# Making modulation blocks on VectorE instead of TensorE in a two-layer trunk, with MLP loops written out and norms applied by a diagonal matrix

## The chip, the cores and the metric

The kernel runs on one core of one Trainium2 chip. The metric is the device time of one execution in microseconds (us); lower is better.

## What is computed

Two layers over 256 latent tokens of width 2048 (D), with 256 context tokens that feed layer 0 alone:

```python
for i in range(2):
    m_lat = split(silu(c)     @ ada_w[i] + ada_b[i], 6)   # shift, scale, gate; shift, scale, gate
    m_ctx = split(silu(c_ctx) @ ada_w[i] + ada_b[i], 6)   # layer 0 only
    hn = rms_norm(h, norm1_g[i]) * (1 + m_lat[1]) + m_lat[0]
    if i == 0:   # one projection (6560 columns) for both head groups, then one output projection
        y = concat(diff_attention(hn @ w_in), rwkv7(hn @ w_in)) @ w_out
    else:        # pointwise 2048->4096, gate, 31-tap depthwise convolution, norm, silu, pointwise
        y = conformer_conv(hn)
    h = h + m_lat[2] * y
    hn = rms_norm(h, norm2_g[i]) * (1 + m_lat[4]) + m_lat[3]
    h = h + m_lat[5] * (square(relu(hn @ mlp_w1[i])) @ mlp_w2[i])
```

The modulation `silu(c) @ ada_w` has 6 chunks of 2048 columns per layer, worked on in blocks of 512 columns: 48 blocks in all, each with 2048 x 512 weights (4 MB). The context's row is needed for layer 0's first two chunks alone.

## The kernel before, in words

All work is written out per engine; each engine runs its queue in order and waits on semaphores. The stages, with their place in the profiled execution: 8 modulation blocks and the first norm (0 to 143 us); the input projection, 13 products of up to 512 columns (143 to 616); 8 attention heads, one modulation block each (650 to 820); the RWKV recurrence, 8 passes of two heads (837 to 1590), called heads here; the output projection, 4 products (1607 to 1697); layer 0's MLP (1718 to 2440); layer 1's convolution module (2468 to 2857), MLP (from 2881) and store.

**Products.** A product's weights come in 4 chunks of 1 MB into `raw`, from SP's queue. ScalarE rounds a chunk into `split_hi` (`act_split`), VectorE subtracts for `split_lo` (`dve_split`), TensorE multiplies. All three buffers are single: a chunk's load waits for both splits of the same chunk of the product before, ScalarE's split for TensorE's end with that chunk of the product before. So ScalarE's split of the last chunk starts when TensorE ends a product. In the input projection ScalarE then evicts banks 0 and 1, VectorE 2 and 3, and ScalarE stores all of them. A chunk takes TensorE 10.9 us, or 5.4 in products 0, 1, 6 and 7.

**Modulation blocks.** The weights are moving operand, the vector `s32` of 32 columns stationary; `pe_ada_chunk` (L361) does four matmuls of a chunk side by side into four partition groups, whose sum is made later by the loads that read it. `act_ada` (L377) copies the bank and stores 4 rows in `mod_scratch`. Blocks 16 to 47 are done in the recurrence, 4 per head: `ada_chunk` at steps 8, 12, 18 and 22 of the inverse (28 steps of transposes L1272, updates L1229, mask L962 on VectorE, copies L728 and L732 on ScalarE) and 12 in the scan (four parts; L1285, L1313, L1330, L1349, L1350, L1298; VectorE L1065). Between the scan's parts work of the next head is done (`rates`, `decays`, `key_norm`, `decay_sums`, `turn`); `scaled_queries` (L921, L924) is VectorE's last work for the next head's first scores (L1212). L1236, the mean of the head before, stands just ahead of these.

**Gates.** Pool makes `gate` (128 x 2048) from the bias and four partition groups, each a load of 1 MB that accumulates and waits for the one before: five loads for each gate, issued when the products that used the gate before have been added (`res_add`). VectorE waits for it (`gate_in`) before the MLP's first split of a next product.

**MLP.** Four quarters, each 4 up products (`pe_joined`, L438 and L440) and 4 down products (`pe_product`, L420), in a hardware loop (`Fori`) on PE, ACT, DVE and SP; layer 1's last quarter is written out on ACT and DVE alone. An up product is evicted by ScalarE (a half copy), VectorE (sum, squared relu, low part), a down product by VectorE (times gate, add to `hbuf`).

**Norms.** `act_stats` squares both token tiles (128 x 2048) with a sum, takes the root; `dve_scale` scales the tiles into `xn2`; TensorE transposes 8 groups of four (L455); `dve_modulate` applies gain and shift; ScalarE and VectorE split.

Of the kernel before, what the change touches and what calls it, by code (L numbers as in the profile page):

```python
# [14 lines left out]
P = 128  # L15
# [113 lines left out]
ADA_A, ADA_T, ADA_R = 8, 1, 4  # L129
Q_AT = ADA_A  # L130
Q_RW = Q_AT + ADA_T * HEADS
Q_ALL = Q_RW + ADA_R * HEADS
# [102 lines left out]
def build_trunk(nc, a, out):  # L235
    with ExitStack() as top:
# [20 lines left out]
        part = line[:, 2:4, :]  # L257
        s32 = sb(top, "s32", [P, KT, 32])
# [11 lines left out]
        epsc = sb(top, "epsc", [P, 2])  # L270
        prow = [hbuf[:, 0, 0:P], hbuf[:, 0, P:2 * P]]
# [6 lines left out]
        with ExitStack() as s:  # L278
# [8 lines left out]
            xa_hi, xa_lo = xa[:, :, 0, :], xa[:, :, 1, :]  # L287
            with ExitStack() as t:
                hT_hi = sb(t, "hT_hi", [P, KT, SEQ], F32R)
                hT_lo = sb(t, "hT_lo", [P, KT, SEQ], F32R)  # L290
            with ExitStack() as t:
                xn2 = sb(t, "xn2", [P, 2, D])
# [15 lines left out]
        ST_T = 16 * HEADS  # L308
        ST_END = [ST_T + 16 * HEADS * (ADA_R // 2), 16 * HEADS * (ADA_R // 2)]
# [6 lines left out]
        norm_sq = sem("norm_sq")  # L316
# [18 lines left out]
        def send(sp, src, n, before):  # L335
# [10 lines left out]

        def rwkv_ada(i, j):

            return (0, i.n(NB, Q_RW * NB)) if j == 0 else (1, i.n((ADA_R - 1) * NB, (j - 1) * NB))

# [30 lines left out]
        def act_split(act, m, b, n=NB):  # L381

            for c in range(NCH):
                act.wait_ge(raw_in[c], b * 16 + 16)
                if not (isinstance(m, int) and m == 0):
                    act.wait_ge(pe_chunk, m * 4 + (c - 3))
                nc.scalar.activation(split_hi[:, c, :, 0:n], raw[:, c, :, 0:n], ACT.Copy).then_inc(hi_done, 1)  # L387

# [68 lines left out]

        def dve_modulate(dve, n0, tiles, cols, hi, lo):
# [54 lines left out]
        def load_mod_rows(pool, m, layer, col):  # L513

            for g in range(4):
                pool.dma_start(mrow[32 * g:32 * g + 32, m, :], rows_of(mod_d[layer, g, col:col + 2 * D])).then_inc(mrow_in, 16)
# [5 lines left out]
        def gate_part(pool, n, l, c, g):  # L522

            pool.wait_ge(gate_in, n * 80 + (g + 1) * 16)
# [39 lines left out]
        def evacuated(m, bank):  # L564

            mine = 0 if bank < 2 else 2
            return sum(1 for n in range(m + 1) for b, *_ in mix_out(n) if mine <= b < mine + 2 and (n < m or b <= bank))

# [80 lines left out]
        def rwkv_act(act, steps):  # L649
# [68 lines left out]
            def ada_rows(x, j):  # L718

                layer, col = rwkv_ada(x, j)  # L720
                slot = 1 - j % 2
                act_ada(act, layer, col, x.n(ADA_R, Q_RW + j), slot, x.n(32, (ST_T, 0)[slot] + 16 * (j // 2)), 0)

# [10 lines left out]
            def scan(x, last):  # L734

                for c in range(4):
# [4 lines left out]
                    if c == 0:  # L741
                        ada_rows(x, 0)
                        if not last:
                            rates(x.next())
                    elif c == 1:
                        if not last:
                            decays(x.next())
                        ada_rows(x, 1)
                        if not last:
                            key_norm(x.next())  # L750
# [3 lines left out]
                    else:  # L754
                        ada_rows(x, 2)
# [4 lines left out]
                ada_rows(x, 3)  # L760
# [373 lines left out]
        def rwkv_pe(pe):  # L1134
# [9 lines left out]
            def ada_chunk(x, n):  # L1144

                j, c = divmod(n, NCH)
                q = x.n(ADA_R, Q_RW + j)
                pe_ada_chunk(pe, q, x.n(ADA_R, Q_RW + MIX_M + j), c, 0, q)

# [106 lines left out]
            def inverse(x, first):  # L1256
# [7 lines left out]
                for k in range(NS + 2):  # L1264
# [13 lines left out]
                    elif k in (8, 12, 18, 22):  # L1278
                        ada_chunk(x, (8, 12, 18, 22).index(k))
# [21 lines left out]
            def scan(x, last):  # L1301
# [6 lines left out]
                for c in range(4):  # L1308
# [9 lines left out]
                    elif c == 1:  # L1318
                        ada_chunk(x, 6)
                        if not last:  # L1320
                            decays(x.next(), 1)
                    elif c == 2:
                        if not last:
                            decay_sums(x.next(), 0)
                        ada_chunk(x, 9)
# [8 lines left out]
                    if c == 0:  # L1334
                        ada_chunk(x, 4)
                    elif c == 1:
                        ada_chunk(x, 7)
                    elif c == 2:
                        if not last:
                            decay_sums(x.next(), 1)  # L1340
                        ada_chunk(x, 10)
                    else:
                        ada_chunk(x, 12)
# [12 lines left out]
                    if c == 0:  # L1356
                        if not last:
                            decays(x.next(), 0)
                        ada_chunk(x, 5)
                    elif c == 1:  # L1360
                        if not last:
                            key_norm(x.next())
                        ada_chunk(x, 8)
                    elif c == 2:
                        if not last:
                            decay_sums(x.next(), 2)
                        ada_chunk(x, 11)
                    else:
# [5 lines left out]
                if not last:  # L1374
                    for n in range(1, 5):
# [41 lines left out]
        diag_a, diag_used = sem("diag_a"), sem("diag_used")  # L1417
        TR0, TR1, TR2 = 16, 24, 32
# [12 lines left out]

        def sync_rest(sp):
# [3 lines left out]

            def mlp(l, m0):
                with sp.Fori(0, Q4) as i:
                    for k in range(4):
                        send(sp, weight_src(a["mlp_w1"][l], i * D + k * NB), NB, src(i * 8 + (m0 + k)))  # L1440
                    for k in range(4):
                        send(sp, weight_src(a["mlp_w2"][l], k * NB, NB, i * D), NB, src(i * 8 + (m0 + 4 + k)))
# [13 lines left out]
        def pool_rest(pool):  # L1456
            stage_end(pool, 3)

            for b in range(2):
                pool.wait_ge(ada_st[b], ST_END[b])  # L1460
            pool.dma_start(line[0:1, 1, :], a["conv_pw2_b"][:, NB:2 * NB]).then_inc(line_in, 16)
# [737 lines left out]
```

## Time and profile before

| | us |
|---|---|
| median of 3 runs | 3624.95 (3624.19 to 3635.03) |
| the profiled execution, its own time | 3620.88 |
| its span, first to last instruction | 3619.2 |
| TensorE busy (PE) | 3290.5 (91%) |
| VectorE busy (DVE) | 1890.1 (52%) |
| ScalarE busy (ACT) | 1364.8 (38%) |
| mean granted TensorE clock | 0.952 of 2.4 GHz |

The profile is one execution recorded by the hardware. PE is TensorE, DVE VectorE, ACT ScalarE, SP and POOL the two engines that issue most of the DMAs; L361 is line 361. In a timeline row stand start, duration, engine, line, operation, what is written and read, count, and in brackets the idle time of the engine before it and what ended that. An fp32 matmul leaves two records, a transpose one. The granted clock is 1.00 at 2.4 GHz and 0.50 at 1.2 GHz.

### The profile page before, as it was taken

What the parts mean: (1) busy time and instruction counts of PE and PEld (TensorE: products, weight loads), DVE (VectorE), ACT (ScalarE), POOL (GpSimd) and SP (SyncE); (2) the same over time, 40 slices, a digit from 0 to 9 for tenths busy, and PEclk for the clock granted to TensorE, in tenths of its full rate; (3) what the DMA queues carried; (4) which work ended last, traced back from release to release, by engine and by line L of the source; (5) the groups of instructions that cost most, each with busy time, mean ns of one, the idle gap of its engine ahead of it and who ended that gap; (6) DMA issues with size and microseconds to landing.
All of it is one profiled execution on the core that took longest, in us unless ns stands there. A gap on an engine that the chain in (4) does not pass through costs nothing.

```text
span 3619.2 us, 48320 instructions
## 1 busy us (share of the span) xinstructions
PE 3290.5 (91%) x19488; PEld 2668.8 (74%) x19488; DVE 1890.1 (52%) x2244; ACT 1364.8 (38%) x1581; POOL 91.3 (3%) x148
## 2 busy tenths in 40 slices
PE   5799998567999999978999999997998899999999
PEld 1588986235777777746888888887986677878787
DVE  0522321666556555535555555555996555555554
ACT  1321220334555555533333343333463333434342
POOL 1000000010000000000000000000000000000000
PEclk8799999678999999989999999998999999999999
DMA  9633531684555555565655655556521565565553
GB/s 357 219 128 127 163 110 51 239 250 136 191 196 195 197 197 193 188 249 189 182 195 184 197 186 189 184 194 180 186 82 58 168 193 194 178 198 175 189 179 132
DMA packets 320206, 651.07 MB, mean 180 GB/s; under 512 B 15499, under 2 KB 20321, under 8 KB 316641
## 3 DMA queue, kind: packets, MB, share of 16 engines
q1 hardware_dynamic: 300000, 597.04, 49.1%
q0 software_dynamic: 8896, 35.95, 4.2%
q10 hardware_dynamic: 11104, 15.01, 1.2%
q8 instruction: 169, 2.77, 0.3%
q14 instruction: 37, 0.30, 0.0%
HBM read 634.22 MB, written 13.60 MB: 179 GB/s over the span
## 4 chain that ended last, share of the span: by engine, by line
PE 83%; DMA 7%; DVE 6%; issue 2%; ACT 1%; ACTq 1%; POOL 0%; SPq 0%; POOLq 0%; DVEq 0%
PE ps L420 42%; PE ps L438 13%; PE ps L440 6%; PE ps L1229 6%; DMA raw<-in_ada_w_dram 4%; PE ps L361 3%; PE ps L1272 3%; PE ps L1785 2%; DMA gate<-mod_scratch 2%; DVE rw_scl L944 1%; PE ps L2167 1%; PE ps L1285 1%; DMA at_qk<-qkv_scratch 1%; PE ps L1330 1%; DVE rw_scc L947 1%
## 5 line engine op out<-in xcount | busy, mean ns | idle before, releaser
L397 DVE TENSOR_TENSOR split_lo<-raw,split_hi 128x2048 fp32r<-128x2048 f32 (+1 forms) x372 | 850.0, 2288 | 1095.3 <-ACT split_hi L387 1049.6
L387 ACT ACTIVATE split_hi<-raw 128x2048 fp32r<-128x2048 f32 (+1 forms) x372 | 710.3, 1911 | 1323.8 <-PE ps L420 974.0
L438 PE MATMUL ps<-xa,split_hi 128*128 128x512 f32 x2048 | 724.7, 398 | 21.2 <-DVE split_lo L397 12.2
L440 PE MATMUL ps<-xa,split_lo 128*128 128x256 f32 x2048 | 576.3, 281 | 9.3 <-issue 9.3
L438 PEld LDWEIGHTS ps<-xa,split_hi 128*128 128x128 f32 x2048 | 388.3, 190 | 125.7 <-issue 35.5
L420 PE MATMUL ps<-split_lo,hT_hi 128*128 128x512 f32 x1024 | 398.4, 389 | 0.0
L420 PE MATMUL ps<-split_hi,hT_lo 128*128 128x512 f32 x1024 | 398.4, 389 | 0.0
L420 PE MATMUL ps<-split_hi,hT_hi 128*128 128x512 f32 x1024 | 398.4, 389 | 0.0
L440 PEld LDWEIGHTS ps<-xa,split_lo 128*128 128x128 f32 x2048 | 390.5, 191 | 0.0
L361 PE MATMUL ps<-raw,s 128*32 128x512 f32 x1536 | 224.3, 675 | 49.4 <-DMA raw<-in_ada_w_dram 49.3
L420 PEld LDWEIGHTS ps<-split_hi,hT_hi 128*128 128x128 f32 x1024 | 192.2, 188 | 40.2
L420 PEld LDWEIGHTS ps<-split_lo,hT_hi 128*128 128x128 f32 x1024 | 192.2, 188 | 39.8
L420 PEld LDWEIGHTS ps<-split_hi,hT_lo 128*128 128x128 f32 x1024 | 192.2, 188 | 39.7
L1229 PEld LDWEIGHTS ps<-rw_tt,rw_mx 128*128 128x128 f32 x1536 | 187.1, 192 | 29.8 <-ACT rw_mx L732 29.2
L1229 PE MATMUL ps<-rw_tt,rw_mx 128*128 128x128 f32 x1536 | 206.4, 278 | 0.0
L728 ACT ACTIVATE rw_tt<-ps 128x512 f32<-128x512 f32 x224 | 133.7, 597 | 164.6 <-PE ps L1229 164.6
L420 PE MATMUL ps<-xa,split_hi 128*128 128x256 f32 x1024 | 186.2, 285 | 6.2 <-DVE tmpa L476 6.2
L420 PE MATMUL ps<-split_hi,xa 128*128 128x512 f32 x512 | 163.0, 398 | 31.0 <-DVE split_lo L397 19.3
L962 DVE TENSOR_TENSOR rw_mb<-rw_tt,rw_lmask 128x512 f32<-128x512 f32 x192 | 132.4, 689 | 96.5 <-ACT rw_tt L728 96.3
L420 PEld LDWEIGHTS ps<-xa,split_hi 128*128 128x128 f32 x1024 | 161.3, 194 | 6.5 <-issue 6.5
L420 PE MATMUL ps<-mx_lo,split_hi 128*128 128x512 f32 (+1 forms) x448 | 157.4, 351 | 0.0
L420 PE MATMUL ps<-mx_hi,split_hi 128*128 128x512 f32 (+1 forms) x448 | 157.3, 351 | 0.0
(328 smaller groups left out, 4408.0 us busy)
## 6 DMA issues: line engine op xcount, KB each, us to landing
raw<-in_mlp_w_dram SPq DMA_DIRECT2D x256, 1024.0 KB, 5.3
raw<-in_ada_w_dram SPq DMA_DIRECT2D x192, 1024.0 KB, 8.1
raw<-in_mix_in_w_dram SPq DMA_DIRECT2D x48, 1024.0 KB, 5.1
raw<-in_conv_pw_w_dram SPq DMA_DIRECT2D x48, 1024.0 KB, 5.2
gate<-mod_scratch POOLq DMA_DIRECT2D x16, 1024.0 KB, 8.3
raw<-in_mix_out_w_dram SPq DMA_DIRECT2D x16, 1024.0 KB, 5.8
qkv_scratch<-hbuf ACTq DMA_DIRECT2D x20, 256.0 KB, 3.8
rwkv_scratch<-hbuf ACTq DMA_DIRECT2D x18, 256.0 KB, 2.2
```

Of the source, the lines that this page charges most:

```text
L361: mm = pe.matmul(ps[32 * kk:32 * kk + 32, ADA_ACC[acc], :], s32[:, c * CHUNK + kk, :], raw[:, c, kk, :], start=(c == 0), stop=(c == NCH - 1))
L387: nc.scalar.activation(split_hi[:, c, :, 0:n], raw[:, c, :, 0:n], ACT.Copy).then_inc(hi_done, 1)
L397: nc.vector.tensor_tensor(split_lo[:, c, :, 0:n], raw[:, c, :, 0:n], split_hi[:, c, :, 0:n], ALU.subtract).then_inc(lo_done, 1)
L420: mm = pe.matmul(dst, l, r, start=(first and i == 0 and opens), stop=(last and i == 2), skip_group_check=True)
L438: pe.matmul(ps[:, base + j, :], split_hi[:, c, kk, j * P:(j + 1) * P], both, start=(k == 0), stop=False, skip_group_check=True)
L440: mm = pe.matmul(ps[:, base + j, 0:SEQ], split_lo[:, c, kk, j * P:(j + 1) * P], xa_hi[:, k, :], start=False, stop=(k == KT - 1), skip_grou ...
L728: nc.scalar.activation(rw["tt"][:, k % 4, :, :], four(ZB[k % 4]), ACT.Copy).then_inc(W["z7"], 1)
L944: ins = V.tensor_tensor(rw["scl"][:, c - 2, inst, :].rearrange("p (q t) -> p q t", q=4), ps[:, SCB[n], :].rearrange("p (q t) -> p q t", q= ...
L962: V.tensor_tensor(dh(rw["mb"][:, k % 2, :, :]), dh(src), bc(rw["lmask"][:, lev, :, :], 2), ALU.mult).then_inc(W["mb"], 1)
L1229: mm = pe.matmul(ps[:, ZB[c], inst * P:(inst + 1) * P], R["mx"][:, k % 2, inst, :], rhs, start=(k < 4 and inst == 0), stop=True, skip_grou ...
L1272: tr = pe.transpose(ps[:, MB[k % 2], inst * P:(inst + 1) * P], R["mb"][:, k % 2, inst, :], ident[:, :])
L1785: mm = pe.matmul(ps[:, j // 2, (j % 2) * SEQ:(j % 2 + 1) * SEQ], diag[:, t % DIAG_SLOTS, j, :], gpad[:, KT - PE_F + j, t:t + SEQ], start=( ...
```

## The change

Four things.

1. The 32 blocks of the recurrence go. Sixteen (layer 0's chunks 4 and 5, layer 1's 0 and 1) are made on VectorE during the input projection, sixteen (layer 1's chunks 2 to 5) during layer 0's MLP. A block is 16 steps on a piece of 128 x 512 (256 KB, one DMA each from SP's queue): `acc = piece * scale + acc` (`piece_step`, `late_step`), each waiting for the one before. Then four small matmuls with ones add up the partitions (`sum_rows`, `late_sum`) at a set chunk of a set product, into the first bank of the next product in the projection; ScalarE copies and stores the row (`keep_rows`, `late_rows`). By the tables `M_STEPS` and `L_STEPS` there are 7 steps a chunk (3 in products 0, 1, 6 and 7) in the projection, 9 a product in the MLP until its 29th. Sums in the projection come before chunks (1,3), (2,3), (3,1), (3,3), (4,1), (5,0), (5,2), (6,0), (7,0), (8,1), (9,0), (9,2), (10,0), (10,3), (11,1), (11,3) (product, chunk); in the MLP before chunk 2 of 16 of the products. Pieces have 7 buffers in the projection and 3 in the MLP.
2. These blocks have one row, not four, so three of the four gates and most modulation rows need one load after the bias, not four.
3. The MLPs are written out on all engines.
4. A norm takes its squares block by block beside the products before it; TensorE multiplies `hbuf` by a diagonal matrix of the reciprocal deviations (`pe_scaled_turns`) in place of scaling and transposing.

```diff
-ADA_A, ADA_T, ADA_R = 8, 1, 4
+ADA_A, ADA_T = 8, 1
+ADA_M, M_BUF = 16, 7
+ADA_L, L_BUF = 16, 3
...
+        def pe_scaled_turns(pe, n0):
+            for i in range(KT // 2):
+                n = n0 + i
+                if n >= 4:
+                    pe.wait_ge(tr_ts, n - 3)
+                for j in range(2):
+                    for t in range(2):
+                        k = 2 * i + j
+                        o = (2 * j + t) * P
+                        mm = pe.matmul(ps[:, n % 4, o:o + P], hbuf[:, t, k * P:(k + 1) * P], rdiag[:, t, :], start=True, stop=True)
+                mm.then_inc(tr_ps, 1)
...
+        def act_squares(act, steps, k, count):
+            act.wait_ge(res_add, count)
+            for t in range(2):
+                steps.link(nc.scalar.activation(sqj[:, :], hbuf[:, t, k * NB:(k + 1) * NB], ACT.Square,
+                                                accum_out=small[:, 18 + 4 * t + k:19 + 4 * t + k]))
...
+        M_STEPS = [0]
+        for m in range(MIX_M):
+            for c in range(NCH):
+                M_STEPS.append(min(M_STEPS[-1] + (3 if m in (0, 1, 6, 7) else 7), ADA_M * KT))
+        M_SUM = {}
+        for b in range(ADA_M):
+            M_SUM[next(j for j in range(len(M_STEPS)) if M_STEPS[j] >= (b + 1) * KT) + 1] = b
...
+        def piece_step(dve, n):
+            b, k = divmod(n, KT)
+            acc, scale = macc[:, b % 2, :], s32[:, k, 0:1]
+            dve.wait_ge(piece_in[n % M_BUF], 16 * (n // M_BUF + 1))
...
+                dve.wait_ge(macc_ok, n)
+                nc.vector.scalar_tensor_tensor(out=acc, in0=piece[n % M_BUF], scalar=scale, in1=acc,
+                                               op0=ALU.mult, op1=ALU.add).then_inc(macc_ok, 1)
...
+        def sum_rows(pe, m, b):
+            pe.wait_ge(macc_ok, (b + 1) * KT)
+            if m >= 1:
+                pe.wait_ge(mix_ev_a, evacuated(m - 1, 0))
+            pe.wait_ge(mrow_ok, b)
+            pe_partition_sums(pe, mix_bank(m + 1, 0), macc[:, b % 2, :]).then_inc(mrow_ps, 1)
...
+        def keep_rows(act, m, b):
+            layer, col = mix_ada(b)
+            act.wait_ge(mrow_ps, b + 1)
+            act.wait_ge(mrow_st, 16 * b)
+            nc.scalar.activation(mline, ps[:, mix_bank(m + 1, 0), 0:P], ACT.Copy).then_inc(mrow_ok, 1)
+            act.wait_ge(mrow_ok, b + 1)
+            store_rows(act, layer, col, mline).then_inc(mrow_st, 16)
...
-                    elif k in (8, 12, 18, 22):
-                        ada_chunk(x, (8, 12, 18, 22).index(k))
...
-                        ada_chunk(x, 13)
                 if not last:
-                    turn(x.next(), 0)
-                ada_chunk(x, 14)
-                ada_chunk(x, 15)
-                if not last:
-                    for n in range(1, 5):
+                    for n in range(5):
                         turn(x.next(), n)
...
+        L_STEPS = [0]
+        for t in range(NCH * 32):
+            L_STEPS.append(min(L_STEPS[-1] + (3 if t % NCH == 0 else 2), ADA_L * KT))
...
+        def load_late(sp, n):
+            b, k = divmod(n, KT)
+            if n >= L_BUF:
+                sp.wait_ge(macc_ok, MIX_STEPS + n - L_BUF + 1)
+            sp.dma_start(lpiece[n % L_BUF], ada_src(1, 2 * D + b * NB)[:, k, :]).then_inc(piece_in[n % L_BUF], 16)
...
+        def late_sum(pe, m, b):
+            i, k = divmod(m, 8)
+            pe.wait_ge(macc_ok, MIX_STEPS + (b + 1) * KT)
+            if k == 0:
+                pe.wait_ge(res_ps, 4 * i + 3)
+                pe.wait_ge(tr_ts, TR0 + 8)
+            elif k < 6:
+                pe.wait_ge(sum_ok, 4 * i + min(k, 4))
+            else:
+                pe.wait_ge(res_ps, 4 * i + 5)
...
                 for c in range(NCH):
                     if m + 1 < MIX_M:
                         dve_split_chunk(dve, m + 1, c, min(NB, IN_COLS - (m + 1) * NB))
+                    for n in range(M_STEPS[4 * m + c], M_STEPS[4 * m + c + 1]):
+                        piece_step(dve, n)
...
                 def bank_free(g, m=m, banks=banks):
+                    if g == 0 and m:
+                        pe.wait_ge(mrow_ok, sum(1 for t in M_INSIDE if t < 4 * m))
...
-            with act.Fori(0, Q4) as i:
-                mlp_quarter(i, M_MLP0, 0, 4, False)
+            for i in range(Q4):
+                mlp_quarter(i, M_MLP0, 0, 4, False, True)
```

## Rows read from the trace of the kernel before

**Rows 1.** The page's part 4: the chain that ended last, by engine.
```profile
PE 83%; DMA 7%; DVE 6%; issue 2%; ACT 1%; ACTq 1%; POOL 0%; SPq 0%; POOLq 0%; DVEq 0%
```

**Rows 2.** Timeline of PE in one head's inverse; then the page's part 5.
```profile
1059.57 0.60 PE L1272 MATMUL ps<-ident_t,rw_mb 128*128 128x128 f32 x4
1060.10 1.06 PE L361 MATMUL ps<-raw,s 128*32 128x512 f32 x8
1062.09 0.60 PE L1272 MATMUL ps<-ident_t,rw_mb 128*128 128x128 f32 x4
1063.42 0.60 PE L1272 MATMUL ps<-ident_t,rw_mb 128*128 128x128 f32 x4
...
L728 ACT ACTIVATE rw_tt<-ps 128x512 f32<-128x512 f32 x224 | 133.7, 597 | 164.6 <-PE ps L1229 164.6
```

**Rows 3.** PE before MLP products: timeline; waits (idle us, count, longest) of 1750:2430, 2930:3619.
```profile
1746.30 0.77 PE L438 MATMUL ps<-xa,split_hi 128*128 128x512 f32 x1 [5.60 <-DVE split_lo L397]
...
PE ps L438 <- issue: 5.9, 6, 1.3
...
PE ps L440 <- issue: 9.3, 3, 3.2
```

**Rows 4.** Timeline of ACT, then of PE, at layer 0's second norm.
```profile
1704.05 1.91 ACT L494 ACTIVATE xn<-hbuf 128x2048 f32<-128x2048 f32 x1 [4.75 <-DVE hbuf L1585]
...
1711.11 4.27 PE L455 MATMUL ps<-ident_t,xn 128*128 128x128 f32 x24 [13.82 <-DVE xn L504]
```

**Rows 5.** One line's instructions: min/median/max ns, first and last start; then PE's timeline.
```profile
L1236 PE MATMUL ps<-rw_o,rw_blk x16: 379/380/483, 947.0 to 1583.8; 128*128 128x256 f32 x16
...
1550.59 1.10 PE L1285 MATMUL ps<-rw_vt,rw_scc 128*128 128x64 f32 x8 [0.69 <-ACT rw_tt L728]
```

**Rows 6.** Timeline of DVE, then of PE, at the end of a scan.
```profile
1121.02 0.42 DVE L1065 TENSOR_TENSOR rw_u<-ps,rw_rh 128x256 f32<-128x256 f32 x1 [2.69 <-PE ps L1330]
...
1128.25 0.42 DVE L924 TENSOR_TENSOR rw_kx<-rw_r,rw_ep 128x256 f32<-128x256 f32 x1
...
1130.71 0.50 PE L1212 MATMUL ps<-rw_kx,rw_bh 64*128 64x128 f32 x4
```

**Rows 7.** Windows: length, busy us (count) PE PEld DVE ACT POOL, PEclk, DMA, GB/s.
```profile
1554.00:1557.00 3.00, 3.00 (x24) 1.22 (x25) 0.00 (x0) 0.00 (x0) 0.00 (x0) 0.50 0.00 0
3254.00:3260.00 6.00, 5.55 (x18) 4.77 (x18) 1.07 (x1) 0.00 (x0) 0.00 (x0) 0.50 0.55 175
1746.30:1751.30 5.00, 5.00 (x15) 4.29 (x16) 5.00 (x3) 0.00 (x0) 0.00 (x0) 0.50 0.80 262
1711.00:1714.00 3.00, 2.89 (x14) 2.89 (x15) 1.79 (x5) 0.63 (x1) 0.17 (x1) 0.50 0.78 117
1714.00:1718.00 4.00, 2.42 (x19) 1.94 (x18) 3.78 (x8) 1.66 (x3) 0.00 (x0) 0.99 0.85 174
```

**Rows 8.** Timeline of DVE: one multiply-add, and a split.
```profile
1121.37 0.74 DVE L904 SCALAR_TENSOR_TENSOR rw_kk<-rw_k,rw_cur,rw_t 128x512 f32<-128x512 f32 x1
...
1743.63 8.90 DVE L397 TENSOR_TENSOR split_lo<-raw,split_hi 128x2048 fp32r<-128x2048 f32 x4 [17.86 <-DMA gate<-mod_scratch]
```

**Rows 9.** Timeline of ACT at the end of a projection product.
```profile
363.32 1.91 ACT L387 ACTIVATE split_hi<-raw 128x2048 fp32r<-128x2048 f32 x1 [8.96 <-PE ps L420]
365.13 1.06 ACT L1911 ACTIVATE hbuf<-ps 128x512 f32<-128x512 f32 x2
```

**Rows 10.** Windows of the opening and of layer 0's MLP, columns as in 7.
```profile
20.00:100.00 80.00, 59.13 (x284) 16.50 (x284) 6.51 (x10) 9.33 (x14) 0.00 (x0) 0.78 1.03 374
1760.00:2430.00 670.00, 664.11 (x3349) 562.90 (x3348) 364.40 (x196) 258.31 (x151) 0.00 (x0) 1.00 0.58 189
```

**Rows 11.** DMA issues: transfer, queue, count, KB each, median us to landing.
```profile
raw<-in_mlp_w_dram SPq DMA_DIRECT2D x256, 1024.0 KB, 5.3
raw<-in_ada_w_dram SPq DMA_DIRECT2D x192, 1024.0 KB, 8.1
at_cos<-in_cos_dram ACTq DMA_DIRECT2D x1, 256.0 KB, 2.6
```

More of the change, by code:

```diff
@@ L257, in build_trunk @@
         part = line[:, 2:4, :]
+        piece = [gate[:, b * NB:(b + 1) * NB] for b in range(4)] + [tmpa[:, b, :] for b in range(2)] + [line[:, 3, :]]
+        macc, mline = line[:, 0:2, :], line[:, 2, 0:P]
         s32 = sb(top, "s32", [P, KT, 32])
@@ L511, in mod_columns, with parts_of, load_mod_rows @@
             mm.then_inc(mt_ps, 1)
[L513 to L516 removed]
+        def parts_of(layer, chunk):
+            return 4 if (layer, chunk) in PARTED else 1
+        def load_mod_rows(pool, m, layer, chunk):
+            for o in range(2):
+                for g in range(parts_of(layer, chunk + o)):
+                    r0, col = 32 * g + 16 * o, (chunk + o) * D
+                    pool.dma_start(mrow[r0:r0 + 16, m, :], rows_of(mod_d[layer, g, col:col + D])).then_inc(mrow_in, 16)
+        GATES = [(0, 2), (0, 5), (1, 2), (1, 5)]
+        GATE_END = [sum(16 + 16 * parts_of(*x) for x in GATES[:n + 1]) for n in range(4)] + [0]
         def gate_bias(pool, l, c):
@@ L567, in evacuated, with mix_ada, pe_partition_sums, store_rows @@
             return sum(1 for n in range(m + 1) for b, *_ in mix_out(n) if mine <= b < mine + 2 and (n < m or b <= bank))
+        def mix_ada(b):
+            return (0, (16 + b) * NB) if b < 8 else (1, (b - 8) * NB)
+        def pe_partition_sums(pe, bank, acc):
+            for g in range(4):
+                mm = pe.matmul(ps[32 * g:32 * g + 32, bank, 0:P], ones[:, 0:32], acc[:, g * P:(g + 1) * P], start=True, stop=True)
+            return mm
+        def store_rows(act, layer, col, rows):
+            return act.dma_start(mod_d[layer, 0, col:col + NB].rearrange("(g n) -> g n", g=4), rows[0:P:32, :])
@@ L754, in scan @@
                     else:
-                        ada_rows(x, 2)
                         if not last:
@@ L1333, in scan @@
                         mm = inputs_of(x, c + 1)
[L1334 to L1343, printed above, removed]
+                    if c == 2 and not last:
+                        decay_sums(x.next(), 1)
                     pe.wait_ge(W["u"], x.n(4, c + 1))
@@ L1417, in build_trunk @@
         diag_a, diag_used = sem("diag_a"), sem("diag_used")
+        MROW_LOADS = sum(parts_of(l, c + o) for l, c in ((0, 3), (1, 0)) for o in range(2))
         TR0, TR1, TR2 = 16, 24, 32
@@ L1547, in act_rest @@
                 act_split(act, M_PW2 + n + 1, M_PW2 + n + 1 + B_OFF)
+                if n:
+                    act_squares(act, steps, n - 1, 20 + n)
             norm(3, TR2)
-            with act.Fori(0, Q4 - 1) as i:
-                mlp_quarter(i, M_MLP1, 16, 24, False)
-            mlp_quarter(Q4 - 1, M_MLP1, 16, 24, True)
+            for i in range(Q4):
+                mlp_quarter(i, M_MLP1, 16, 24, i == Q4 - 1)
         def dve_rest(dve, steps):
@@ L1622, in dve_rest @@
             norm(1, TR0, 0)
-            dve.wait_ge(gate_in, 160)
-            with dve.Fori(0, Q4) as i:
+            dve.wait_ge(gate_in, GATE_END[1])
+            for i in range(Q4):
                 mlp_quarter(i, M_MLP0, 0, 4, False)
@@ L1741, in mlp, with rows_kept, free @@
             def mlp(m0, abase, rbase, tr0):
-                with pe.Fori(0, Q4) as i:
-                    for k in range(4):
-                        def free(k=k):
+                for i in range(Q4):
+                    for k in range(8):
+                        r = 8 * i + k
+                        def rows_kept(r=r):
+                            if m0 == M_MLP0 and sum(1 for x in L_SUM if x < r):
+                                pe.wait_ge(mrow_ok, ADA_M + sum(1 for x in L_SUM if x < r))
+                        def free(i=i, k=k):
+                            rows_kept()
                             if k == 0:
@@ L1833, in _, with pieces @@
                 n = min(NB, IN_COLS - m * NB)
-                send(sp, weight_src(w["in"], m * NB, n), n, ("product", m - 1) if m else ("ada", ADA_A - 1))
+                def pieces(c, m=m):
+                    if m == 1 and c == 0:
+                        sp.wait_ge(tr_lo, 16)
+                        sp.wait_ge(col_ps, ADA_A)
+                        sp.wait_ge(pt_ok, 1)
+                        for k in range(M_BUF):
+                            load_piece(sp, k)
+                    elif m > 1:
+                        t = 4 * (m - 2) + c
+                        for k in range(M_STEPS[t] + M_BUF, min(M_STEPS[t + 1] + M_BUF, ADA_M * KT)):
+                            load_piece(sp, k)
+                send(sp, weight_src(w["in"], m * NB, n), n, ("product", m - 1) if m else ("ada", ADA_A - 1), pieces)
+            for k in range(M_STEPS[4 * (MIX_M - 2)] + M_BUF, ADA_M * KT):
+                load_piece(sp, k)
             sp.wait_ge(hi_done, 4 * MIX_M)
```

250 lines of the change are left out of this document (170 added, 80 removed).

## The prediction

> **What bounds the kernel now.** I read the page first. TensorE holds 83% of the chain that ended last [rows 1]. So a change pays where it takes work from TensorE or closes one of its pauses, and costs where it makes TensorE wait. Next, the timeline of one head of the recurrence: TensorE goes from one instruction to the next without a pause, a step of the inverse takes 1.33 us (1062.09 to 1063.42), and the step with a modulation chunk 2.52 us (1059.57 to 1062.09) [rows 2]. Then the pauses of TensorE outside: 5.60 us at the second product of layer 0's MLP (and 6.64 at the same place of layer 1's, the second of two such rows), about 1 to 3 us at each loop turn of the MLPs [rows 3], 13.8 us before the transposes of a norm, of which there are three [rows 4]. VectorE has time to spare, but the moved work must fit into its gaps in the projection and in layer 0's MLP.
>
> **A. 32 blocks leave the recurrence.** A head takes (1583.8 - 947.0) / 7 = 91.0 us [rows 5] and holds 16 chunks. Four in the inverse cost 2.52 - 1.33 = 1.19 each, 4.8 us: without them ScalarE's two copies (0.60 each [rows 2]) still fit into 1.33. Eight in the scan's first three parts cost 1.0 each (the chunk's 1.06 less its overlap with the next [rows 2]); what follows was always ready earlier, except once behind ScalarE's square root: 7.7 us. At the scan's end VectorE takes over: from its sum at 1121.02 to its last product, over at 1128.67, run 7.65 us, and the next scores can't start earlier; today they come 9.7 us after that sum [rows 6]. That part gives 2.0 us, not 4. Together 14.5 us a head, times 7. The last head has nothing of a next head to fill its scan. It runs 32.9 us from 1550.59 to 1583.4 [rows 5], the last chunks waiting for their DMA. I count its instructions with 0.7 us for each hop over ScalarE or VectorE: 20.4 us, so 12.5 less, plus 4.8 in the inverse, minus 4 for the clock: it fell to half right there, at 1554 to 1557, after two short waits [rows 7]. **A = -(101.5 + 13.3) = -115.** Bounds: every chunk free and every DMA wait gone, -135; only half of each scan chunk and nothing at the end, -70.
>
> **B. 16 blocks in the projection.** The multiply-add has its shape in the trace: 0.74 us, and 0.03 until one that needs it can start, 0.775 a step [rows 8]. A full chunk gets 7: 5.4 + 2.2 for the split = 7.6 us of VectorE against 10.9 of TensorE; a 256-column chunk or one of the first two products gets 3: 4.5 against 5.4. That fits. The waits don't. A sum is a matmul set in TensorE's queue, and the bank it writes is freed by an eviction that ScalarE does only after the split of the last chunk, which TensorE's own end of product releases: start 363.32, evicted at about 365.7, TensorE's chunk before ended at about 363.1, so 2.5 us [rows 9]. By the code's tables five sums stand at chunk 0 (products 5, 6, 7, 9, 10) and wait for that; five at chunk 3 (1, 2, 3, 10, 11), and the next product then waits for ScalarE's copy of them, behind the same split: 2.35 us, one more after the others. With the first sum late by up to 7 us, since its pieces start late, and 16 sums at 0.3 us (between nothing, beside other work, and 1.0, an old chunk), that is 11 x 2.4 + 3 + 4.8 = 34 us. Pauses of this size lower the clock sometimes: after one of 3.2 us it was at half from 3254 to 3260 [rows 7]; I add 8. VectorE's piece steps also stand ahead of its evictions, for whose end ScalarE's stores wait; with three chunks in hand the splits stand that. **B = +42**, from +20 (pauses half as long, no clock) to +60.
>
> **C. 16 blocks in layer 0's MLP.** A product lasts about 22 us. VectorE has 4 splits (8.9 [rows 8]), two or three operations over half a split's columns (1.2 each), and now 9 steps (7.0): 18.3 to 19.5 us, 86%, from 54% [rows 10]. DMA goes from 189 GB/s to 189 + 2.36 MB / 22 us = 296, against 374 in the opening, where it is full [rows 10]. Only three buffers hold pieces: a load is issued when the step three before is done, and lies in one queue behind 1 MB of weights. A 1 MB load lands in 5.3 us, a 256 KB one alone in 2.6 [rows 11]; behind the other I reckon 5.3 + 0.7 and then 0.7 more for the second, 6.0 and 6.7 us. VectorE wants the first of them about 6.2 us after the split while on time, but 3.8 to 4.6 once it is late, so it can't catch up after each eviction. Followed through chunk by chunk this gives 1 to 3 us of waiting a product; VectorE then needs 21 to 23 us against 22, and TensorE waits at its sums, which ask for VectorE's eviction of the product before. **C = +27** (4.8 for the sums, 22 for waits), from +5, all hidden, to +65, at 0.7 us longer landings and less speed.
>
> What a piece costs in flight is also in the Trainium skill ("DMA: Bandwidth & Descriptors", Anatomy of one DMA): some 2.0 us fixed, plus the bytes. As an estimate from that page a 256 KB piece is 2.7 us, and my sum would be the same; the 2.6 us row agrees.
>
> **D. The gates.** In both MLPs VectorE stood before the gate's parts (17.86 us in layer 0), and TensorE then idled 5.60 and 6.64 [rows 3, 8]. With one part instead of four the gate is there some 25 us earlier. Behind it nothing is late: the norm ends before. The clock was at half for some 5 us after each [rows 7], which costs 2.6. **D = -17.4**; bounds -12 and -18.
>
> **E. Loops written out.** TensorE's pauses at turns are all put down to issue: 5.9 us in six pauses in layer 0; in layer 1 three long ones of 9.3 us together and three short ones like layer 0's, 3. The clock fell after two of the long ones, 5 us [rows 3, 7]. The projection is written out and shows no such pause. **E = -23**, at worst -8 if fetching instructions beside more DMA costs again.
>
> **F. Norms.** From the first square (1704.05) to the transposes (1711.11) 7.1 us: two squares of 1.9, root, reciprocal, two scalings of all of x [rows 4]. Now one block's squares, a quarter of that and their fixed part (2 x 0.9), root, and two small scalings: 3.6 us. The matmul costs two passes where the transpose has one, so the first group comes 0.9 us later, more at the low clock. **F = -6** for three, between -10 and +1.
>
> The Trainium skill ("TensorE: Matmul & The Clock Gate", Part 4) says that transposes don't count as activity for the clock; by it matmuls instead would bring the clock up sooner and F would be nearer -10. The trace speaks against it: with nothing but transposes run, the clock went from 0.50 to 0.99 within the norm [rows 7]. F stands as it is.
>
> **Nothing** for the small loads of modulation rows, the squares on ScalarE (idle 60% of the MLP) and the start of the output projection: there the load of x, issued after the yT copies, is last to arrive in both versions.
>
> **Sum**: -115 + 42 + 27 - 17 - 23 - 6 = -92. The profiled execution took 3620.9 us (span 3619.2), 4 below the median of 3625.0; against the mean of both I predict **3531 us**.
>
> **Rivals.** (1) *The clock falls in every scan.* The old chunks were TensorE's densest work there; the last head shows a fall. Against it: seven heads keep the next head's work as filling. Price: some 8 us a head, 56: 3587. Chance 0.08. (2) *The scan's chain of hops sets the pace*: the chunks hid it, each is worth half. A is -75: 3571. 0.10. (3) *Slower than before*: with three buffers a round of three steps lasts a landing plus a step. If, in the fuller queue, pieces land like the 1 MB modulation loads did, 8.1 us [rows 11], a product with its three rounds takes 3 x 8.9 = 26.7 us, 4.7 more over 28.4 products: C = +134, 3638. It decides from about 6.5 us of landing on (22 / 3 less a step), and reaches the old time near 7.9. 0.07. (4) *Little of B and C shows*: 20 and 5 us: 3487. 0.13. The forecast, 3500 to 3565, has the rest, 0.62.
>
> The skill's same page warns ("Why this matters for your kernels") that pauses between bursts of matmuls take the clock down; that is rival 1, which removing filling invites. If it held for every scan the time would be the 3587 above.
>
> **How the numbers follow.** The range leaves out rival 3 and the edge of rival 4: 3483 to 3592. A measurement can tell about 0.3%, 11 us, from no change. Slower: 0.07. Within: 0.03, between rivals 2 and 3. Faster: 0.90.
>
> **What would show it.** A: heads of 77 us, TensorE waiting for VectorE's last scaled query at their end. B: eleven pauses of 2.4 us at product edges. C: VectorE's steps waiting for DMA, TensorE's for sums, a stage longer by 20 us. D and E: no pauses at the second products and at quarter edges. F: 3.6 us in place of 7.1. It is wrong if the granted clock falls in the heads, if heads stay above 80 us, or if layer 0's MLP grows past 60 us.

## The result, and the profile after

The changed kernel takes 3597.23 us (median of four runs, 3593.53 to 3598.71) against 3628.34 for the kernel before beside it. The ratio is 0.9915, 95% interval 0.9898 to 0.9932: about 0.85% faster, some 31 us, where 92 were forecast. The two profiled executions differ by 22.6 us of span (3619.2 and 3596.6), and the table takes that apart. A stage lasts from TensorE's first instruction of its kind to the first of the next.

| stage | before | after | difference | the prediction had |
|---|---|---|---|---|
| projection, up to attention | 507.6 | 552.9 | +45.3 | +42 (B) |
| attention | 185.5 | 191.2 | +5.6 | 0 |
| recurrence, up to the output projection | 770.4 | 662.5 | -108.0 | -115 (A) |
| output projection, up to norm 1's transposes | 103.9 | 99.2 | -4.8 | part of F |
| norm 1, layer 0's MLP, up to norm 2 | 743.1 | 802.0 | +58.9 | +13 (C 27, part of D and E -14), part of F |
| norm 2, convolution module, up to norm 3 | 420.3 | 420.0 | -0.3 | part of F |
| norm 3, layer 1's MLP, end | 744.7 | 725.1 | -19.6 | -26 (rest of D and E), part of F |

Of the 69 us between -92 and -22.6, some 46 lie in one stage: layer 0's MLP. First the page of the changed kernel: the chain that ended last by engine (before: rows 1), the group of the late multiply-adds with its idle time, and the loads of pieces with their median time to landing.

```profile
PE 66%; DMA 13%; DVE 13%; issue 5%; ACT 2%; ACTq 1%; SPq 0%; POOL 0%; POOLq 0%; DVEq 0%
...
L1541 DVE SCALAR_TENSOR_TENSOR line<-line,cvec 128x512 f32<-128x512 f32 x160 | 119.9, 750 | 96.8 <-DMA line<-in_ada_w_dram 91.1
...
line<-in_ada_w_dram SPq DMA_DIRECT2D x207, 256.0 KB, 5.5
```

TensorE's share of the chain fell from 83 to 66%, and DMA and VectorE rose to 13% each. Now the changed kernel's windows, columns as in rows 7: the projection, one head, the last head's scan, layer 0's MLP, layer 1's MLP.

```profile
143.75:662.45 518.70, 492.79 (x2432) 409.69 (x2432) 309.74 (x329) 106.56 (x88) 0.00 (x0) 0.98 0.70 246
982.50:1059.64 77.14, 72.45 (x654) 64.43 (x653) 54.64 (x106) 44.76 (x82) 4.77 (x8) 1.00 0.05 13
1496.66:1525.52 28.86, 24.22 (x185) 20.81 (x185) 4.60 (x15) 1.53 (x4) 0.00 (x0) 0.60 0.01 1
1658.54:2441.66 783.12, 735.95 (x3715) 616.94 (x3713) 563.44 (x474) 290.74 (x223) 0.00 (x0) 0.96 0.75 254
2880.50:3596.60 716.10, 710.28 (x3587) 601.99 (x3585) 386.27 (x217) 269.88 (x160) 0.00 (x0) 1.00 0.56 179
```

Three stages hold idle time and low clock that the kernel before has not to this degree: layer 0's MLP, where TensorE is busy for 736 of 783 us at a mean clock of 0.96; the projection, 493 of 519 us at 0.98; and the last scan, at 0.60 (0.95 before, 1550.59 to 1583.40). TensorE's timeline shows what idles: two of eleven pauses in the projection, the transposes of norm 1, two of eight long pauses in the MLP. Behind them VectorE's and SyncE's timelines of one down product, in which late pieces show.

```profile
193.77 0.47 PE L430 MATMUL ps<-split_hi,mx_hi 128*128 128x512 f32 x1 [2.43 <-ACT line L684]
336.31 0.43 PE L633 MATMUL ps<-line,ones_t 128*32 128x128 f32 x8 [2.59 <-issue]
1649.49 9.29 PE L478 MATMUL ps<-rdiag,hbuf 128*128 128x128 f32 x64 [9.72 <-DVE rdiag L503]
1768.61 0.66 PE L633 MATMUL ps<-line,ones_t 128*32 128x128 f32 x8 [7.16 <-DVE tmpa L1772]
1889.60 0.66 PE L633 MATMUL ps<-line,ones_t 128*32 128x128 f32 x8 [7.89 <-issue]
```

```profile
1999.15 2.29 DVE L407 TENSOR_TENSOR split_lo<-raw,split_hi 128x2048 fp32r<-128x2048 f32 x1
2002.70 1.61 DVE L1541 SCALAR_TENSOR_TENSOR line<-line,cvec 128x512 f32<-128x512 f32 x2 [1.27 <-DMA line<-in_ada_w_dram]
2004.23 2.28 DVE L407 TENSOR_TENSOR split_lo<-raw,split_hi 128x2048 fp32r<-128x2048 f32 x1
2006.43 0.75 DVE L1541 SCALAR_TENSOR_TENSOR line<-late,cvec,line 128x512 f32<-128x512 f32 x1
2008.45 0.75 DVE L1541 SCALAR_TENSOR_TENSOR line<-line,cvec 128x512 f32<-128x512 f32 x1 [1.27 <-DMA line<-in_ada_w_dram]
2009.12 2.29 DVE L407 TENSOR_TENSOR split_lo<-raw,split_hi 128x2048 fp32r<-128x2048 f32 x1
2011.32 0.75 DVE L1541 SCALAR_TENSOR_TENSOR line<-line,cvec 128x512 f32<-128x512 f32 x1
2014.68 0.75 DVE L1541 SCALAR_TENSOR_TENSOR line<-late,cvec,line 128x512 f32<-128x512 f32 x1 [2.62 <-DMA late<-in_ada_w_dram]
2015.35 1.22 DVE L1744 TENSOR_TENSOR tmpa<-ps,gate 128x1024 f32<-128x1024 f32 x1
```

```profile
2006.59 0.38 SPq L355 DMA_DIRECT2D raw<-in_mlp_w_dram  x1
2007.20 0.33 SPq L1528 DMA_DIRECT2D late<-in_ada_w_dram  x1
```

VectorE waits three times in this product, 5.2 us together, each time for a piece. The load of the last `late` piece is issued at 2007.20, when the step three before is over, and its multiply-add starts at 2014.68, 7.5 us on; this landing is a long one, the median is 5.5. The evictions (L1744) come behind that wait, and the sums on TensorE (L633) behind the evictions: the row at 1768.61 names VectorE's L1772, and the "issue" of 7.89 us at 1889.60 ends when the same L1772, begun at 1888.28 and 1.22 us long, is over.

The heads came out as forecast. One line of the source view answers rows 5, one line of TensorE's waits (total, count, longest) names what is last at a head's end:

```profile
L1338 PE MATMUL ps<-rw_o,rw_blk x16: 379/382/794, 982.5 to 1526.1; 128*128 128x256 f32 x16
...
PE ps L1314 <- DVE rw_kx L1032: 7.0, 7, 1.0
```

Six of the seven distances between means are 77.1 to 77.2 us, at full clock; the last is 80.1.

### The profile page after: what moved, and what is told of

Same layout as the page of the kernel before. It is cut to its first block, busy times and chain, and to the rows that moved or that the text cites. A ratio compares the mean times of both kernels' runs of the same rounds, so it can differ in the third digit from the quotient of the medians.

```text
span 3596.6 us, 46596 instructions
## 1 busy us (share of the span) xinstructions
PE 3223.9 (90%) x18816; PEld 2689.8 (75%) x18816; DVE 2240.7 (62%) x2761; ACT 1367.6 (38%) x1653; POOL 81.3 (2%) x136
## 4 chain that ended last, share of the span: by engine, by line
PE 66%; DMA 13%; DVE 13%; issue 5%; ACT 2%; ACTq 1%; SPq 0%; POOL 0%; POOLq 0%; DVEq 0%
PE ps L430 35%; PE ps L448 7%; PE ps L1331 6%; DMA late<-in_ada_w_dram 5%; DMA line<-in_ada_w_dram 4%; PE ps L450 4%; DVE line L1541 3%; PE ps L1374 3%; DMA raw<-in_ada_w_dram 2%; PE ps L1972 2%; ACT split_hi L395 1%; PE ps L1385 1%; PE ps L1428 1%; DVE rw_scl L1052 1%; PE ps L2383 1%
## 5 line engine op out<-in xcount | busy, mean ns | idle before, releaser
L448 PE MATMUL ps<-xa,split_hi 128*128 128x512 f32 x2048 | 735.8, 403 | 0.0
L430 PE MATMUL ps<-xa,split_hi 128*128 128x256 f32 x1024 | 186.7, 285 | 5.7 <-DVE tmpa L524 5.7
L1541 DVE SCALAR_TENSOR_TENSOR line<-line,cvec 128x512 f32<-128x512 f32 x160 | 119.9, 750 | 96.8 <-DMA line<-in_ada_w_dram 91.1
```

The costliest lines, as they stand in the source:

```text
L430: mm = pe.matmul(dst, l, r, start=(first and i == 0 and opens), stop=(last and i == 2), skip_group_check=True)
L448: pe.matmul(ps[:, base + j, :], split_hi[:, c, kk, j * P:(j + 1) * P], both, start=(k == 0), stop=False, skip_group_check=True)
L1541: nc.vector.scalar_tensor_tensor(out=acc, in0=lpiece[n % L_BUF], scalar=scale, in1=acc, op0=ALU.mult, op1=ALU.add).then_inc(macc_ok, 1)
```

## The experiments

The question was what holds up layer 0's MLP, then what the projection, the loops and the last scan each cost. All but one were run once, beside the kernel before; stages are read from their traces. How much a stage scatters shows where the code is the same: norm to norm, layer 0's MLP took 802.0 us in the changed kernel and 805.8 and 797.0 in experiments 7 and 10, which don't touch it.

**1. No loads.** In layer 0's MLP each buffer is loaded once; the steps read it again and again.

```diff
-            sp.dma_start(lpiece[n % L_BUF], ...).then_inc(piece_in[n % L_BUF], 16)
+            if n < L_BUF:
+                sp.dma_start(lpiece[n % L_BUF], ...).then_inc(piece_in[n % L_BUF], 16)
```

> The changed kernel with the pieces of layer 0's MLP loaded only three times, once into each buffer; every multiply-add and every sum stays, so the kernel leaves out the true weights of layer 1's last four modulation chunks. From the first transposes of the norm before this MLP to those of the norm behind it the stage takes 802 us in the changed kernel, 743 before. Theory (pieces land too late): VectorE's 152 us of waiting for pieces make it late at the sums; without them the eight pauses of 3.4 to 8.5 us (46.5 together) and the falls of the clock behind them go, and the stage takes 740 to 752. Rival 1 (VectorE's work is too much as it is, 19 us of 22): the stage stays above 780. Rival 2 (the sums stand too early, whatever VectorE waits for): about half of the pauses stay, 770.

Measured: 3531.9 us; norm to norm 735.3. In the window of the MLP (columns as in rows 7) TensorE is never idle and the clock is full:

```profile
1661.23:2377.42 716.19, 716.19 (x3715) 602.30 (x3713) 565.15 (x474) 292.55 (x223) 0.00 (x0) 1.00 0.57 185
```

All 256 multiply-adds and 16 sums are still there. So neither VectorE's work nor the sums' place costs anything to speak of alone; the waits for pieces, with what follows from them, cost 67 us. Both rivals fall.

**2. Sums one chunk later.**

```diff
-                            if m0 == M_MLP0 and c == 2 and r in L_SUM:
+                            if m0 == M_MLP0 and c == 3 and r in L_SUM:
```

> The changed kernel with each sum of layer 0's MLP before chunk 3 of its product, not chunk 2; pieces load as before. TensorE then gives VectorE 5.4 us more. Theory (VectorE with its waits is slower than TensorE, so it falls back until something stops TensorE): the pauses move or shrink little, the stage takes 785 to 802. Rival (only the sums' place is wrong): pauses of 3.4 to 8.5 us lose 5.4 each, the stage takes 755 to 765.

Measured: 3585.1 us; the stage 795.0, with 16 pauses of together 40.5 us in place of 9 of 47.2. Five of them, 7.8 us together, are new waits of the next product for ScalarE's copy of the row, which now stands behind a later split; some of the others now stand before the splits. The 7 us gained are little more than the scatter. TensorE is stopped by VectorE's pace, and a later sum mostly moves where: the rival falls.

**3. A fourth buffer.** A piece may be loaded into `s32`, not used any more by then; the squares' scratch moves to `rdiag`, the summed row's to a small buffer of its own.

```diff
-ADA_L, L_BUF = 16, 3
+ADA_L, L_BUF = 16, 4
...
-            lpiece = [line[:, 2, :], line[:, 3, :], late[:, :]]
+            lpiece = [line[:, 2, :], line[:, 3, :], late[:, :], s32[:, :, :].rearrange("p k n -> p (k n)")]
```

> The changed kernel with four buffers for pieces in layer 0's MLP, not three. Theory (pieces land too late): a load is issued one step earlier, some 2.4 us, VectorE's 152 us of waiting fall under 40, and the stage falls from 802 to 740 to 760. Rival (DMA's throughput, not its latency, is the limit): the waits stay over 100 and the stage over 785.

Measured: 3526.2 us; the stage 735.1 and no pause. VectorE's waits in that stretch, of the changed kernel and then of this one (total, count, longest; the buffer `s` is the fourth), and this one's window of the MLP:

```profile
DVE line L1541 <- DMA line<-in_ada_w_dram: 91.1, 56, 3.8
DVE line L1541 <- DMA late<-in_ada_w_dram: 53.4, 25, 4.7
```

```profile
DVE line L1543 <- DMA line<-in_ada_w_dram: 18.4, 15, 3.4
DVE line L1543 <- DMA late<-in_ada_w_dram: 10.1, 8, 3.8
DVE line L1543 <- DMA s<-in_ada_w_dram: 9.7, 9, 1.7
...
1655.14:2371.30 716.16, 716.16 (x3715) 602.63 (x3713) 564.11 (x474) 292.62 (x223) 0.00 (x0) 1.00 0.82 278
```

The same bytes come in less time, 278 GB/s in place of 254, though a single piece now lands later (median 6.4 to 6.7 us in that stretch, not 5.5). So it was the time of one landing against too few buffers, not throughput.

**4. Two buffers.**

```diff
-ADA_L, L_BUF = 16, 3
+ADA_L, L_BUF = 16, 2
```

> The changed kernel with two buffers for pieces in layer 0's MLP, not three. Theory (latency of one round): two steps need at least a landing and a step, 5.5 + 0.75 = 6.25 us, so 9 steps of a product need 28 us and more against 22, and the stage between the norms grows from 802 to 900 to 980. If the waits were one of throughput, two buffers would load no more bytes and the stage would stay under 830.

Measured: 3689.6 us; the stage 892.7, a little under the forecast. Pieces landed sooner with fewer in flight, in a median of 5.0 us, where the forecast had put 5.5. The stage by buffers: 892.7 with two, 802.0 with three, 735.1 with four, 735.3 without loads.

**5. The same steps at a lower rate**, three buffers.

```diff
-            L_STEPS.append(min(L_STEPS[-1] + (3 if t % NCH == 0 else 2), ADA_L * KT))
+            L_STEPS.append(min(L_STEPS[-1] + (3 if t % 16 == 0 else 2), ADA_L * KT))
```

> The changed kernel, three buffers, with the same 256 steps of layer 0's MLP spread over 31 products, 8.25 each, not 9 over 28.4. Theory (the round sets VectorE's pace): in the changed kernel's trace one buffer's steps follow each other every 7.7 us (five rounds from 1998.5 to 2037.1), so 9 steps need 3 x 7.7 = 23.1 us and TensorE's product takes some 22.3; 8.25 need 21.2, VectorE catches up, and the stage between the norms falls from 802 to 740 to 765. Rival (each step carries its own wait of 0.6 us, whatever the rate): the same sum of waits, 790 to 802.

Measured: 3558.2 us; the stage 765.9, pauses 23.6 us. But the waits stayed:

```profile
DVE line L1541 <- DMA line<-in_ada_w_dram: 90.0, 59, 3.3
DVE line L1541 <- DMA late<-in_ada_w_dram: 47.2, 29, 3.5
```

My theory, by which three rounds of 7.7 us set VectorE's pace, falls: VectorE did not catch up and the waits did not vanish, as the rival said, while the time was nearer to mine. What does add up in both kernels is VectorE's time for one product. Four splits (9.2), the eviction (3.6, the mean of up and down products, with the wait for ScalarE's half), 9 steps (6.8) and 152 us of waits over 28.4 products (5.4) make 24.9 us; measured, (802.0 - 735.1) / 28.4 = 2.4 over TensorE's 22.3, which is 24.7. With 8.25 steps and 145 us over 31 products it is 9.2 + 3.6 + 6.2 + 4.7 = 23.7; measured 22.3 + (765.9 - 735.1) / 31 = 23.3. The waits in these sums are read from the traces, so they account for the pace and don't forecast it. A reading that fits, and is argued only: as long as the sum is over 22.3, VectorE stays late, and a late VectorE asks for every piece too soon.

**6. Pieces from a queue of their own**, GpSimd's, so that none stands behind a 1 MB chunk in SyncE's.

```diff
+                if n == 4:
+                    pool.wait_ge(mt_ps, 1)
+                    for x in range(ADA_L * KT):
+                        load_late(pool, x)
```

> The changed kernel, three buffers, with the pieces of layer 0's MLP loaded from GpSimd's queue and not from SyncE's, where each stands behind a weight chunk of 1 MB and its wait. Theory A (a piece lands late because it lies behind 1 MB in its queue): landings fall from 5.5 to 3 to 4 us and the stage from 802 to 740 to 765. Theory B (the engines that all queues share are what is slow): landings stay over 5 and the stage over 785.

Measured: 3587.0 us; the stage 790.7. The loads in the MLP (1660 to 2400 us) in the changed kernel, then the pieces here:

```profile
raw<-in_mlp_w_dram SPq DMA_DIRECT2D x119, 1024.0 KB, 6.6
line<-in_ada_w_dram SPq DMA_DIRECT2D x169, 256.0 KB, 5.5
...
line<-in_ada_w_dram POOLq DMA_DIRECT2D x169, 256.0 KB, 5.1
late<-in_ada_w_dram POOLq DMA_DIRECT2D x85, 256.0 KB, 5.2
```

Landings shrink by 0.3 to 0.4 us, and GpSimd issues a load a median of 0.29 us after the step that frees its buffer, where SyncE took 0.03. Theory A falls: the place in SyncE's queue is not what makes a piece late. One rival is left: the profile counts GpSimd's queue as of another kind (software_dynamic, not hardware_dynamic), which may have a cost of its own, and ScalarE's queue was not tried. A 256 KB load with no 1 MB load beside it took 2.6 us [rows 11], and the 1 MB loads slowed too, from a median of 5.3 to 6.6. That fits engines that all loads share; no run takes it apart further.

**7. The projection's sums away from the edges.** Sums of chunk 0 stand at chunk 1; for chunk 3 ScalarE copies the row ahead of its split.

```diff
-            M_SUM[next(j for j in range(len(M_STEPS)) if M_STEPS[j] >= (b + 1) * KT) + 1] = b
+            j = next(j for j in range(len(M_STEPS)) if M_STEPS[j] >= (b + 1) * KT) + 1
+            M_SUM[j + 1 if j % NCH == 0 and j < NCH * MIX_M else j] = b
```

> The changed kernel with the projection's sums away from product edges: those of chunk 0 stand at chunk 1; for those of chunk 3 ScalarE copies the row before it splits the last chunk, not behind. The projection takes 518.7 us in the changed kernel, 473.2 before. Theory (each edge pause is TensorE behind ScalarE's split): the eleven pauses of 1.4 to 2.6 us go (27 us), and the clock falls with them, 483 to 492. Rival (VectorE's load or the pieces' DMAs stop TensorE next): pauses come back at the splits, above 505.

Measured: 3570.1 us; from the first product to attention 524.9 (552.9), three pauses left, 6.0 us together. (The expectation's 483 to 492 is for the products without the load and norm behind them, 34.2 us: it answers to 517 to 526.) Eight of eleven pauses are gone. Two of the three left are sums that stand one chunk behind another sum, whose copy ScalarE makes only after a split: the same cause.

**8. Four buffers, and all row copies ahead of the splits.** Experiment 3 with this in the projection, and the first sum two chunks later:

```diff
-            act_split(act, m + 1, ADA_A + m + 1, min(NB, IN_COLS - (m + 1) * NB), lambda c, m=m: rows_at(m, c))
+            act_split(act, m + 1, ADA_A + m + 1, min(NB, IN_COLS - (m + 1) * NB), None, lambda c, m=m: rows_at(m, c))
...
         def act_split(act, m, b, n=NB, behind=None, ahead=None):
             for c in range(NCH):
+                if ahead:
+                    ahead(c)
```

> Four buffers for pieces in layer 0's MLP, and in the projection: the sums of chunk 0 at chunk 1, the first sum two chunks later, and ScalarE copies every summed row before the split it stood behind. Four buffers alone gave 3526 us with a projection of 552.5 us up to attention; moved sums alone gave one of 524.9 with three pauses left, 6.0 us together. If the two add up and the three pauses go too, the projection comes to 516 to 522 and the whole to 3488 to 3502. Rival: earlier work of the projection delays the copies or loads of what follows, 3505 or more.

Measured: 3494.3 us (3489.4 to 3499.1), ratio 0.9632 with the interval 0.9605 to 0.9659. No pause is left in the projection (517.3 us up to attention) nor in layer 0's MLP (736.2). This version beats both kernels, by 3.7% and about 2.9% (the second from medians that were not measured side by side). It stands near the forecast's 3487 of rival 4. Of the 108.9 us by which its profiled execution is shorter than the changed kernel's, 101.4 lie in these two stages (35.7 and 65.7): what B and C had lost in waits.

**9. Only the loops written out**, on the kernel before.

```diff
-            with act.Fori(0, Q4) as i:
+            for i in range(Q4):
```

> The kernel before with only the MLPs' loops written out on all engines. The prediction's step E: the pauses at loop turns, 5.9 us in layer 0 and 12.3 in layer 1, and some 5 us of low clock go, 23 together: from norm to norm 743.1 becomes 737, from the third norm to the end 739.0 becomes 722, the whole 3598 to 3606. Rival: fetching the instructions costs again, the whole over 3612.

Measured: 3608.0 us; layer 0's stage 735.0 (743.1), from norm 3's transposes on 730.2 (744.7; the expectation's 739.0 leaves out the transposes), together -22.7. The turns' pauses are gone; what is left of TensorE's pauses in the products is one at each second product, where VectorE waits for the gate:

```profile
1753.92 0.76 PE L438 MATMUL ps<-xa,split_hi 128*128 128x512 f32 x1 [3.73 <-issue]
...
2911.50 0.77 PE L438 MATMUL ps<-xa,split_hi 128*128 128x512 f32 x1 [6.01 <-issue]
```

**10. Filling for the last scan.** Ten groups of four matmuls of 32 x 512 on constants, used by nobody, in the last head's scan of the changed kernel.

```diff
+                if last:
+                    for kk in range(4):
+                        pe.matmul(ps[32 * kk:32 * kk + 32, 4, :], s32[:, kk, :], R["smask"][:, 0, :], start=True, stop=True)
```

> The changed kernel with ten groups of four matmuls of 32 x 512 on constants (1.06 us each) in the last head's scan, where chunks had stood; their result is used by nobody. In the changed kernel that scan takes 28.9 us with the clock at half for 20.5 of them. If the clock falls for want of work, it stays at full, the scan's own work shortens by some 8 us and the fill costs up to 10: 28 to 33 us, no gain. If the clock falls for another reason, the scan takes 35 us or more.

Measured: 3593.1 us. The scan's window, after the one of the changed kernel shown above:

```profile
1498.56:1527.69 29.13, 28.17 (x264) 16.19 (x264) 4.60 (x15) 1.53 (x4) 0.00 (x0) 0.88 0.00 1
```

With ten more groups of matmuls in it the scan takes 29.1 us, not 28.9, and the mean clock is 0.88, not 0.60. So the clock had fallen for want of work on TensorE; the filling brought back what it cost, no more.

## Why the prediction was wrong

The direction was right; the size was not: 3597 us lies above the 3592 that the range ended with, and the gain was a third of the one forecast.

**C failed, and with it the forecast.** The part cost about 73 us, where I had +27, at worst +65: 67 for the waits, which experiments 1 and 3 gave back, and 6.1 for the sums (16 at 0.38 us, read in experiment 3). The table agrees: the stage grew by 58.9, although the loops gave back 8.1 there (experiment 9), the gate's pause with its clock some 5 and the shorter pause at norm 2 4.0, while norm 1's matmuls took 1.9 more; that makes 74. The sums were nearly right (4.8 forecast). The step that failed is the term of the waits, 22 us from "1 to 3 us of waiting a product": it measured 5.4 us a product, and nothing was set aside for the clock. I had the right pieces: a late VectorE wants its next piece 3.8 us after the load is issued (a step, a split, a step), a landing takes 5 to 6. I even wrote that it can't catch up after an eviction, and still counted too few waits. The rows of 1999 to 2015 show three waits of 1.3 to 2.6 us in one product, and over the MLP there are 96 in 28.4 products. With 5.4 us in place of 1 to 3, my own 18.3 to 19.5 us of work come to at most 24.9 against TensorE's 22.3: 2.6 us over 28.4 products, some 74 us, where 67 came. Of these 67, 47.2 are pauses at sums and the other 20 the clock, at 0.96 instead of 1.00 in the stage; B had a term for that, C none.

**Rival 3 was the right mechanism with the wrong threshold.** It put the round at a landing and a step and said that it decides from 6.5 us of landing on. It decided at 5.5: a piece that has landed still waits for what VectorE is at, a median of 1.5 us, and one buffer's steps followed each other every 7.7 us (1998.5 to 2037.1, five rounds; 8.0 is the median over the MLP), not every 6.25. By experiment 5 even this round is no fixed pace. The estimate that the prediction took from the Trainium skill ("DMA: Bandwidth & Descriptors", Anatomy of one DMA) changed nothing: the section gives its fixed 2.0 us for loads that GpSimd issues, and by its 436 GB/s 256 KB come to 2.6 us, an estimate, not 2.7. C turned on the landing among 1 MB loads, 5.5 us.

**A: nearly right.** A head takes 77.15 us from mean to mean, 77 forecast, with the wait for the scaled query where it was expected. Rival 1, the clock falling in every scan, did not come: 1.00 in the heads. It came in the last one, which has no next head to fill it. From the last mean but one to the output projection 111.6 us became 104.9, -6.6 where -13.3 stood; the scan took 28.9 us, not 24.4, with the clock at 0.60. The 4 us set aside for the clock were too few, and experiment 10 confirms the cause.

**B: right, +45.3 for +42.** Eleven pauses, most of 2.4 to 2.6 us, at the chunks named (the first sum's is 1.35, where "up to 7" stood). Without them (experiment 8) 9.6 us stay, where 16 sums at 0.3 had been 4.8; pauses (25.9) and clock make up the other 35.7.

**D and E: right within some 6 us.** E alone gave -22.7 for -23, but 1.9 of them are part of the gate's first pause, which went with the loops, from 5.60 to 3.73 us. D then had 3.7 and 6.0 us of pause left and some clock to take, by estimate 12 to 13 and not 17. **F: right.** From the first square to the matmuls 2.9 us (1646.59 to 1649.49), where 3.6 stood, the pause of TensorE 4.1 shorter, the matmuls 1.9 longer until the first product, so -2.1 for a norm and -6 for three. On this the trace was rightly believed and not the Trainium skill's sentence ("TensorE: Matmul & The Clock Gate", Part 4) by which transposes don't count as activity for the clock, so that matmuls in their place would have brought it up sooner: from the start of the transposes to the first product norm 1 now takes 9.05 us at 0.82, before 7.1 at 0.79.

**Attention**, +5.6, has the same instructions in both kernels, and the granted clock differs: in nine experiments on the changed kernel the stage took 185.8 to 190.4 us, in the changed kernel itself 191.2, in the kernel before 185.5 and with its loops written out 186.7. Most of the 5.6 is that scatter; whether 2 or 3 us of it are the change's stays open.

## What to carry to other kernels

Work moved to an engine with time to spare needs its data on time as well: count for each buffer the time from the load's issue to its use *when the engine is late*, and compare that with a landing in traffic, not with one on an idle chip. If work and waits together exceed the pace of the engine that bounds, the lateness seems to feed itself, and one more buffer is worth more (67 us here) than all else that the change brought but the recurrence. And where an in-order engine waits for another's copy, put the copy ahead of that engine's long work: eleven pauses of 2.4 us cost 36 us with the clock they took down.

## What the runs showed of the hardware

- A load of 256 KB among 1 MB loads landed in a median of 5.0 us with two buffers, 5.5 with three and 6.4 to 6.7 with four, and with three in 5.1 to 5.2 from GpSimd's queue; with no 1 MB load beside it one took 2.6 [rows 11]. The traffic changed the landing much, the queue little.
- In layer 0's MLP nine pauses of 0.7 to 8.5 us, 47 us in all, cost 67: 20 us more in clock. In the projection eleven of 1.3 to 2.6 us, 26 in all, cost 36. In the last scan no pause was over 0.9 us, and the clock was at half for 20.5 us from 1499.24 on.
- A scan with small matmuls and short waits ran at a mean clock of 0.60 and took 28.9 us; with ten groups of useless matmuls between it ran at 0.88 and took 29.1. There, work that filled TensorE was free.
